# The rows of the activation buffer `hs` lie 2080 bytes apart instead of 2048

## The reference

```python
h = rmsnorm(x, norm_pre_mix)
m = hgrn2_mixer(h, hgrn_w_in, ...)          # h @ w_in: 2048 -> 10240, recurrence, @ w_out
x = x + rmsnorm(m, norm_post_mix)
h = rmsnorm(x, norm_pre_ffn)
x = x + rmsnorm(conv_ffn(h, ffn_w_in, ffn_w_conv, ffn_w_out), norm_post_ffn)   # 2048 -> 11264, 5632 -> 2048
```

```python
h = rmsnorm_2(x, mix_norm);  proj = h @ w_in            # 2048 -> 7184
x = x + concat(stick_breaking_attention(...), gated_deltanet(...)) @ w_out
x = x + memory_cross_attention(rmsnorm_2(x, xattn_norm), rmsnorm_2(mem, mem_norm), w_xq, w_xkv, w_xo)
x = x + conv_ffn_2(rmsnorm_2(x, ffn_norm), w_up, ffn_conv, ffn_conv_bias, w_down)   # 2048 -> 11264, 5632 -> 2048
return rmsnorm_2(x, final_norm)
```

## Time and profile before

| | |
|---|---|
| median of 3 runs | 2696.56 us (2696.28 to 2697.19) |
| profiled execution, its own time | 2697.01 us |
| its span, from the first to the last instruction | 2695.2 us |
| granted TensorE clock, mean | 0.999 of 2.4 GHz |
| TensorE products, busy | 2683.5 us (100%), 17616 instructions |
| stationary loads, busy | 2291.9 us (85%) |
| VectorE busy | 1971.6 us (73%) |
| ScalarE busy | 1335.3 us (50%) |
| HBM traffic | 178 GB/s over the span |

### The profile page before, as it was taken

One profiled execution on the slowest core, in us unless ns is written; L12 is line 12 of the kernel. 1 busy time (PEld: TensorE's weight loads), 2 busy tenths in 40 slices (PEclk: granted clock), 3 DMA queues, 4 the chain that ended last, 5 costly groups with the idle time before them and its releaser, 6 DMA issues.

```text
span 2695.2 us, 47424 instructions
## 1 busy us (share of the span) xinstructions
PE 2683.5 (100%) x17616; PEld 2291.9 (85%) x17616; DVE 1971.6 (73%) x2721; ACT 1335.3 (50%) x1679; POOL 133.9 (5%) x138
## 2 busy tenths in 40 slices
PE   9999999999999999999999999999999999999998
PEld 8888888888888888888888888878888888888887
DVE  6888888878888888644466677767678888885444
ACT  6455555455444444433465566665644444443443
POOL 0211121210000000000000000000000000000000
PEclk9999999999999999999999999999999999999999
DMA  7555555475555555655645544355455555556554
GB/s 245 180 165 172 165 168 173 161 196 170 189 187 187 187 187 187 195 187 187 218 139 181 170 145 139 134 171 186 150 190 187 187 187 187 187 188 197 185 184 150
DMA packets 136197, 481.68 MB, mean 179 GB/s; under 512 B 14880, under 2 KB 19120, under 8 KB 135680
## 3 DMA queue, kind: packets, MB, share of 16 engines
q1 hardware_dynamic: 134160, 472.06, 53.2%
q0 software_dynamic: 1376, 7.46, 0.8%
q10 hardware_dynamic: 528, 0.26, 0.0%
HBM read 477.63 MB, written 2.10 MB: 178 GB/s over the span
## 4 chain that ended last, share of the span: by engine, by line
PE 82%; DVE 8%; issue 4%; DMA 3%; ACT 2%; DVEq 1%; SPq 0%; ACTq 0%
PE acc L442 29%; PE acc L444 15%; PE acc L465 8%; PE acc L467 8%; PE acc L466 8%; PE acc L414 4%; DMA raw<-stream 3%; DVE wts L362 3%; PE acc L415 2%; ACT wts L355 2%; DVE cy L2313 2%; DVE cin L392 1%; DVE half L380 1%; PE ps L1406 1%; PE ps L740 1%
## 5 line engine op out<-in xcount | busy, mean ns | idle before, releaser
L442 PE MATMUL acc<-hs,wts 128*128 128x512 f32 x4640 | 1626.8, 394 | 0.0
L362 DVE TENSOR_TENSOR wts<-raw,wts 128x1024 fp32r<-128x1024 f32 x888 | 1061.9, 1227 | 525.0 <-ACT wts L355 524.3
L355 ACT ACTIVATE wts<-raw 128x1024 fp32r<-128x1024 f32 x888 | 913.6, 1055 | 847.0 <-PE acc L444 367.9
L444 PE MATMUL acc<-hs,wts 128*128 128x256 f32 x4640 | 1297.1, 280 | 0.0
L442 PEld LDWEIGHTS acc<-hs,wts 128*128 128x128 f32 x4640 | 871.0, 188 | 194.1 <-DVE wts L362 0.9
L444 PEld LDWEIGHTS acc<-hs,wts 128*128 128x128 f32 x4640 | 871.5, 188 | 0.5
L467 PE MATMUL acc<-wts,acts 128*128 128x512 f32 x688 | 272.8, 396 | 0.0
L465 PE MATMUL acc<-wts,acts 128*128 128x512 f32 x688 | 272.6, 396 | 0.2 <-DVE wts L362 0.2
L466 PE MATMUL acc<-wts,acts 128*128 128x512 f32 x688 | 270.4, 393 | 0.0
L369 ACT ACTIVATE half<-acc 128x512 f32<-128x512 f32 x161 | 95.3, 592 | 157.7 <-PE acc L444 138.9
L466 PEld LDWEIGHTS acc<-wts,acts 128*128 128x128 f32 x688 | 129.2, 188 | 32.2
(11 more groups left out here) (361 smaller groups left out, 2172.7 us busy)
## 6 DMA issues: line engine op xcount, KB each, us to landing
raw<-stream SPq DMA_DIRECT2D x888, 512.0 KB, 4.1
xf<-xT SPq DMA_DIRECT2D x8, 256.0 KB, 6.6
raw<-stream SPq DMA_DIRECT2D x8, 256.0 KB, 6.7
fm<-memT POOLq DMA_DIRECT2D x2, 1024.0 KB, 6.6
fw<-stream POOLq DMA_DIRECT2D x2, 1024.0 KB, 10.7
memr<-memT POOLq DMA_DIRECT2D x1, 2048.0 KB, 9.8
outT<-memr SPq DMA_DIRECT2D x7, 256.0 KB, 2.8
KQ<-masks POOLq DMA_DIRECT2D x1, 448.0 KB, 5.7
```

Source lines behind the costliest of these rows:

```text
L355: nc.scalar.activation(high, source, ACT.Copy).then_inc(hi_ready, 1)
L362: nc.vector.tensor_tensor(low, source, high.bitcast(F32), ALU.subtract).then_inc(lo_ready, 1)
L442: nc.tensor.matmul(acc[:, 2 * par + n, :], whi[:, b, c:c + P], src[:, kt, :], start=start, stop=False)
L444: mm = nc.tensor.matmul(acc[:, 2 * par + n, 0:T], wlo[:, b, c:c + P], src[:, kt, 0:T], start=False, stop=stop)
```

## The change

The buffer `hs` gets 520 numbers a row instead of 512, and the program goes on using the first 512 of each. Row `kt` begins at 2080 x kt instead of 2048 x kt bytes behind the start of `hs`, which stays where it was. `hs` is thereby 33280 bytes long, 512 more than `hold`, so a buffer of 512 bytes is declared behind `hold` that nothing uses. All buffers declared after it begin 512 bytes later; their own rows keep their distance. 2080 is 65 x 32, so over the 16 rows the start goes through all 16 multiples of 32 within 512 bytes.

```diff
         with ExitStack() as st:
-            hs = sb("hs", [P, DT, 2 * T], F32R, st)
+            hs = sb("hs", [P, DT, 2 * T + 8], F32R, st)[:, :, 0:2 * T]
         with ExitStack() as st:
             memr = sb("memr", [P, DT, T], F32, st)
             m = sb("m", [P, DT, T], F32, st)
         mt = m[:].rearrange("p (f c n) t -> p f c (n t)", f=4, c=2)
         grow = memr[:, DT // 2:].rearrange("p a t -> p (a t)")
         hold = sb("hold", [P, DT, 2 * T])
+        sb("below_hs_end", [P, 8 * DT])
```

## The result

| | before | after |
|---|---|---|
| median of 4 runs each | 2696.88 us (2696.28 to 2698.88) | 2713.39 us (2712.34 to 2714.70) |
| ratio | 1 | 1.0059, 95% interval 1.0046 to 1.0072 |
| profiled execution, span | 2695.2 us | 2711.7 us |

The change makes the kernel 16.5 us slower. The forecast was 2696.6 us, no change, with a range from 2689 to 2705. It was wrong: the kernel got slower, and the time lies above the range.

What follows compares the result with a forecast made beforehand. The prediction took TensorE's products, busy 2683.5 of 2695.2 us, to bound the kernel. All terms were taken as 0, so the sum was 0 and the forecast the median, 2696.6 us, with a range of 2689 to 2705.

Steps and rivals of the forecast that it cites:

- What bounds the kernel: Whole kernel: TensorE's products, busy 2683.5 of 2695.2 us; time is their number times the distance between starts.
- the price list: Pairs of products that read `hs`: 0.2% of the time, 5.4 us over 5056 pairs, is 1.07 ns a pair.
- TensorE reads rows of `hs` that begin 32 x kt bytes later ... I take 0 ns a pair, since this row is the nearest: Products moving `hs` rows: shifted starts cost 0 ns a pair, judged by the `spp` product; bounds -21.7 to +29 ns.
- the bound: Upper limit for pairs reading `hs`: stationary loads set the pace, 376 ns a pair, +29 ns, 147 us more.
- The rival of the two streams: Moving and stationary streams collide today; new distance frees 21.7 ns a pair, 101 us, to 2596 us; chance 0.11, full or part.
- The 325 ns a pair: Pairs of L442 and L444: estimated pace without collision, from plain float32 products, against 346.7 ns in the trace.
- The slower rival: Odd `hs` rows, now on multiples of 64, cost 3.5 ns more, +8.1 us; 0.09 together with other small-offset costs.
- The shift of the other buffers: Everything above `hold` moves by 512 bytes and keeps its place within 512; taken as 0.
- The writes of ScalarE and VectorE: Writes of `hs` rows at L752, L1010 and L759: one run in one row each; taken as 0.
- The stationary pieces of `hs`: L414 and L415, 384 pairs loading `hs` as stationary operand: same argument, a twelfth of the moving rows' price.
- What would show it: Test in L442's windows: 1095 and 1155 products again if right; wrong if distance of starts depends on `kt`.

Runs made afterwards that it cites:

- the faster version: The kernel before the change with `os_`, `mixs`, `xs` and `acts` 96 bytes later, `hs` and weights where they were; 2679.53 us, ratio 0.9939.

## Why the prediction was wrong

*What bounds the kernel* was right: each ns in the distance of TensorE's starts came out in the time, 17.1 us of distances and 16.5 us of time. So was the price list, 5.4 us for 1.07 ns a pair.

*"TensorE reads rows of `hs` that begin 32 x kt bytes later ... I take 0 ns a pair, since this row is the nearest"* is the step that failed. The term measures 17.1 us / 4640 = +3.7 ns a pair. Its first half held, read as steps that are multiples of 512 bytes: they do nothing, and the pattern repeats even after 256. Rows 1 and 9 of the changed kernel, 256 bytes apart within 512, both take 359 ns. The second half rested on one row with another place, the product with `spp`. I compared its place with that of `hs`, which differ by 128 bytes. What counts is the place against the stationary operand, and I didn't work that out: `sums_r` begins at byte 181376, `spp` at 209568, the difference within 256 is 32. That of `hs` against the weights is 160. These are two of the three good places in the table whose rows agree, and they are 128 apart. That the one row that I took as a sample lay at another good place was chance, and it could say nothing about the places between. I should have written that no row shows a difference of 32 to 96 bytes from the fast places, and left the whole stretch up to the bound open instead of giving it 9 in 100.

*The rival of the two streams* named the right pair of operands and the wrong sign: `hs` already lay at one of the good places, and the change moves 12 of the 16 rows off the two good ones that it knows, 160 and 32. Its argument against itself ("a collision would come and go") tested only shifts by multiples of 512 bytes, which are none within 256. The 325 ns a pair were never reached: no place had a pace clearly under that of before.

*The slower rival* had the sign, and 8 us instead of 16.5. Its mechanism is wrong: odd rows, on multiples of 64, should have been slow and even ones not, but `kt` 3 takes 345.4 and `kt` 6 354.0 ns; and with everything 32 bytes later the pattern stayed. What it saw in the slower forms was real, though: the out- and down-projections did lie at a bad difference, and that is the 17 us of the faster version. For L414 and L415 no run shows what a place is worth.

*The shift of the other buffers* at nothing: right, by the run with the shift alone (ratio 1.000). *The writes of ScalarE and VectorE* at nothing: L759 takes 477 ns after and 478 before. *The stationary pieces of `hs`*: 160.5 us before, 159.6 after, a small gain.

*What would show it* named the right test: "wrong if the distance of starts depends on `kt` at all".

## What to carry to other kernels

In a kernel like this one, where TensorE is the bound with a load of the stationary operand for each product, the start of the moving operand minus that of the stationary one, within 256 bytes, is a parameter to try: it was worth 17 of 689 us, 2.5%, of the out- and down-projections here, for an unused buffer of 96 bytes in front of each operand. Read it from the distance of starts in a stretch without waits, form by form, since the two forms here have different good differences, and a change in one place can win in one form what it loses in another and leave the time as it was. Take the difference from the addresses in the built program, not from the sizes in the source: here an unused buffer of 80 bytes moved the next one by 96. And one row that agrees is a sample only if what it varies is the quantity that counts.

## What the runs showed of the hardware

How fast `float32r` products follow each other depends on where the moving operand begins against the stationary one, within 256 bytes. With the same instructions, the pair took 346.8 to 354.5 ns by place, the same with `hs` moved by 96 (352.5) as with the weights moved by 160 (352.1), and the out- and down-projections' product 226.8 to 234.3; with both moved together by 32 bytes nothing changed. It made no difference whether ScalarE and VectorE wrote beside the products. The Trainium skill, "SBUF — State Buffer", section "Who interferes with whom", says that the two use ports of their own and that TensorE waits for no one; the pace here does depend on the two together. That it is their reads which meet is the likely reading, but no run shows the reads themselves.

Not shown is which load the moving row meets (by the run with the low weights moved, the place of the high pieces counts for most), why the differences 16, 32 and 160 are fast in one form and 0 in the other, and why several places settle in patterns of two or three distances, such as 340, 343 and 357 ns.
